# Gated feed-forwards that take the unnormalised residual, with token factor and shift applied behind the PSUM banks

## The reference, cut to what matters

```python
for l in range(DEPTH):                       # DEPTH = 2, SEQ = 256, D_MODEL = 1024
    ...
    y = hybrid_mixer(h, positions, ...)
    x = x + g_m * rms_norm_2(y, mix_norm_post[l])
    h = rms_norm_2(x, ffn_norm_pre[l]) * (1.0 + sc_f) + sh_f
    y = swiglu(h, w_gate_up[l], w_down[l])   # FFN_HIDDEN = 2816
    x = x + g_f * rms_norm_2(y, ffn_norm_post[l])

def rms_norm_2(x, w):
    return x * lax.rsqrt(jnp.mean(x * x, axis=-1, keepdims=True) + EPS) * w

def swiglu(h, w_gate_up, w_down):
    g, u = jnp.split(h @ w_gate_up, 2, axis=-1)
    return (jax.nn.silu(g) * u) @ w_down
```

## Time and profile before

| | |
|---|---|
| median of 3 runs | 2164.08 us (2161.91 to 2165.92) |
| the profiled execution's own time | 2163.82 us |
| its span in the trace | 2161.9 us |
| PE busy | 2004.4 us, 93% |
| DVE busy | 1521.2 us, 70% |
| ACT busy | 907.6 us, 42% |
| POOL busy | 142.3 us, 7% |
| mean granted TensorE clock | 0.959 of full speed |

### The profile page before, as it was taken

The page is one execution under the profiler, slowest core; times in us unless marked ns, Lnnn a source line. Parts: engine busy times, 40 slices in busy tenths (PEclk is TensorE's granted clock), DMA queues, the critical chain, the costliest instruction groups (busy, mean ns, idle before and its releaser), DMA issues. The chain is left out here.

```text
span 2161.9 us, 39923 instructions
## 1 busy us (share of the span) xinstructions
PE 2004.4 (93%) x16706; PEld 1788.0 (83%) x16706; DVE 1521.2 (70%) x2353; ACT 907.6 (42%) x1355; POOL 142.3 (7%) x231
## 2 busy tenths in 40 slices
PE   6998988999999889899999999799899979999997
PEld 5786765788888678798888999789789979988997
DVE  6866557798777668765647787689776667966454
ACT  2435453222222244423225444456544345554443
POOL 0100000001010001201210000000000000000000
PEclk7999989999999989999999999799999999999999
DMA  8542013356453176200004777343358744323552
GB/s 326 203 145 78 2 59 136 136 176 213 161 200 145 58 255 211 104 4 3 3 3 156 250 269 272 127 165 126 136 189 285 270 152 157 136 99 120 192 177 95
DMA packets 59132, 323.92 MB, mean 150 GB/s; under 512 B 6384, under 2 KB 7536, under 8 KB 32624
## 3 DMA queue, kind: packets, MB, share of 16 engines
q1 hardware_dynamic: 33360, 228.97, 29.7%
q0 software_dynamic: 25344, 92.29, 12.0%
q10 hardware_dynamic: 288, 0.66, 0.1%
HBM read 320.84 MB, written 1.05 MB: 149 GB/s over the span
## 5 line engine op out<-in xcount | busy, mean ns | idle before, releaser
L370 DVE TENSOR_TENSOR w_low<-raw,w_high 128x1024 fp32r<-128x1024 f32 (+1 forms) x408 | 473.4, 1202 | 196.9 <-ACT w_high L362 196.7
L362 ACT ACTIVATE w_high<-raw 128x1024 fp32r<-128x1024 f32 (+1 forms) x408 | 402.6, 1034 | 363.0 <-PE banks L407 352.3
L548 DVE SCALAR_TENSOR_TENSOR mod_rows<-mod_rows,silu_condition 128x1024 f32<-128x1024 f32 x176 | 212.9, 1221 | 9.0 <-DMA mod_rows<-rows_dram 6.3
L405 PE MATMUL banks<-ffn_a_l,w_high 128*128 128x256 f32 x704 | 201.1, 286 | 8.5 <-DVE ffn_a_l L712 6.5
L406 PE MATMUL banks<-ffn_a_h,w_high 128*128 128x256 f32 x704 | 199.3, 283 | 0.0
L407 PE MATMUL banks<-ffn_a_h,w_low 128*128 128x256 f32 x704 | 199.1, 283 | 0.0
L534 POOL DMA_DIRECT2D mod_rows<-rows_dram x176 | 93.2, 530 | 1329.7 <-DVE mod_rows L548 1108.6
L405 PE MATMUL banks<-mlp_hidden_l,w_high 128*128 128x512 f32 (+1 forms) x512 | 174.7, 341 | 3.9 <-DVE mlp_hidden_l L1102 3.0
L407 PE MATMUL banks<-mlp_hidden_h,w_low 128*128 128x512 f32 (+1 forms) x512 | 174.5, 341 | 0.0
L406 PE MATMUL banks<-mlp_hidden_h,w_high 128*128 128x512 f32 (+1 forms) x512 | 174.4, 341 | 0.0
L405 PE MATMUL banks<-mix_l,w_high 128*128 128x256 f32 (+1 forms) x448 | 134.4, 300 | 14.0 <-DVE mix_l L759 12.9
(11 more groups left out here) (617 smaller groups left out, 4983.3 us busy)
## 6 DMA issues: line engine op xcount, KB each, us to landing
raw<-panels_dram SPq DMA_DIRECT2D x204, 1024.0 KB, 4.8
mod_rows<-rows_dram POOLq DMA_DIRECT2D x176, 512.0 KB, 5.1
mod_0a_rows<-rows_dram SPq DMA_DIRECT2D x8, 1024.0 KB, 19.3
x_features<-x_features_dram SPq DMA_DIRECT2D x1, 2048.0 KB, 11.2
constants<-small_dram SPq DMA_DIRECT2D x1, 1672.5 KB, 6.7
silu_condition<-conditions_dram SPq DMA_DIRECT2D x2, 512.0 KB, 12.4
out_dram<-x_features SPq DMA_DIRECT2D x4, 256.0 KB, 2.1
constants<-small_dram SPq DMA_DIRECT2D x1, 736.5 KB, 5.1
```

Source lines behind the costliest of these rows:

```text
L362: self.nc.scalar.activation(self.wh[:, m % 2, cols], self.raw[:, slot, cols], ACT.Copy).then_inc(self.w_high, 1)
L370: self.nc.vector.tensor_tensor(self.wl[:, m % 2, cols], self.raw[:, slot, cols], self.wh[:, m % 2, cols].bitcast(F32), ALU.subtract).then_ ...
L405: self.nc.tensor.matmul(out, sh(k), ml(k), start=(opens and k == 0), stop=False)
L548: nc.vector.scalar_tensor_tensor(row if v == nv - 1 else self.scratch[:], row, 1.0, self.cond[v][:], ALU.mult, ALU.mult, accum_out=mod[:, ...
```

## The change

For each gated feed-forward:

- `norm_modulate` ahead of it goes. A `Deferred` object prepares the operand: ACT writes `x * gain` rounded to the high part and squares x, DVE writes the low part. Its small gain and shift work is done beside the first `mix_out` panel.
- In `post_add` POOL does the 8 products `y * r`; DVE keeps the 8 additions to x and does the 8 low parts between them. The two halves of the second panel's split go into `post_add` too.
- The matmuls have 258 columns. In chunk 0 PE goes block by block through both banks of the gate panel and sums the squares of x between them; then it does the up panel. DVE multiplies both halves by `r` on the way out of the banks, ACT adds the gate's shift in the silu, DVE adds the up half's shift in the product.
- Banks 5 to 7 are opened ahead of `post_add`'s sums, bank 4 (which the sums use first) after up(1).
- In the first layer `row_work` is cut into 4 and 28 rows, so that POOL's products stand between them.

The diff, cut to its core:

```diff
+        def pe_up_gated_first(pe):
+            d, ms = deferred, [m_of["up", 0, u] for u in range(2)]
+            with_x = ((0, 0), (0, 1))
...
+            for k in range(KD):
+                pe.wait_ge(d.split, k + 1)
+                for u, b in with_x:
+                    last = half_product(0, ms[u], u, b, k, k == 0, k == KD - 1)
...
+                d.pe_sum(pe, k, 4)
+            self.wait_split(pe, ms[1])
+            for b in range(len(with_x) - 2, 2):
+                for k in range(KD):
+                    last = half_product(0, ms[1], 1, b, k, k == 0, k == KD - 1)
+            last.then_inc(up_done, 1)
...
+        def dve_up_gated(dve, cs, q=None):
...
+            dve.wait_ge(up_done, 2 * c + 1)
+            nc.vector.tensor_copy(bias[:], ps[:, 0:2, n:n + 1]).then_inc(bias_ready, 1)
+            nc.vector.tensor_tensor(act_buf[:], ps[:, 0:2, 0:n], spread(deferred.r[:], 1, 2),
+                                    ALU.mult).then_inc(scaled_ready, 1)
+            dve.wait_ge(up_done, 2 * c + 2)
+            nc.vector.tensor_copy(up_bias[:], ps[:, 2:4, n:n + 1]).then_inc(up_bias_ready, 1)
+            nc.vector.tensor_tensor(hid[:], ps[:, 2:4, 0:n], spread(deferred.r[:], 1, 2),
+                                    ALU.mult).then_inc(up_scaled, 1)
...
+            for b in range(2):
+                last = nc.vector.scalar_tensor_tensor(hid[:, b, :], hid[:, b, :], up_bias[:, b, :], act_buf[:, b, :],
+                                                      ALU.add, ALU.mult)
...
             def body(pe, cs, q):
                 pe_up(pe, cs + 1, q)
+                if deferred is not None and gated and cs == 0:
+                    pe.wait_ge(deferred.rooted, 1)
+                    self.open_sums(pe, (4,))
                 pe_down(pe, cs, q)
...
+            if deferred is not None and gated:
+                self.split_upto("dve", dve, first + 1)
+                deferred.dve_rstd(dve)
+            if deferred is None or not gated:
+                self.split_upto("dve", dve, first + ups)
+            dve_up(dve, 0)
             self.split_upto("dve", dve, first + ups)
-            dve_up(dve, 0)
...
+            @pr.block.gpsimd
+            def _(pool):
+                for w in r_ready:
+                    pool.wait_ge(*w)
+                for k in range(KD):
+                    nc.gpsimd.tensor_tensor(scaled[:, k, :], y[:, k, :], r[:, 0, :], ALU.mult).then_inc(normed, 1)
...
+                pr.open_sums_first()
+                post_add(pr, "mix_post", out_y[:], [], mod, 16, norm("mix_post", l), 4, out_sq,
+                         squared=(squared, (folded, 5), [6, 0, 7]), operand=operand)
...
-                pr.open_sums_first()
-                a_ready = pr.norm_modulate("ffn_pre", norm("ffn_pre", l), mod, 1, 24, 32, TL, high, low,
-                                           lambda k: [(added[0][0], k + 1)], bank=3, scaled_x=y, split_first=1)
```

More of the change, by code:

```diff
@@ L979, in feed_forward, with half_product @@
         up_banks = lambda cs: slice(0, 2) if cs == 0 else slice(first_bank, first_bank + 2)
+        up_scaled, up_bias_ready = (self.sem(f"{name}_{s}") if deferred is not None and gated else None
+                                    for s in ("up_scaled", "up_shift_product_ready"))
+        up_bias = self.sb(f"{name}_up_shift_product", [P, 2, 1], ctx=tmp) if gated else None
+        def half_product(cs, m, u, b, k, first, last):
+            d, out = deferred, ps[:, 2 * u + b, 0:n + 2]
+            cols = slice(k * PC + b * P, k * PC + (b + 1) * P)
+            nc.tensor.matmul(out, self.wh[:, m % 2, cols], d.low[:, k, :], start=first, stop=False)
+            nc.tensor.matmul(out, self.wh[:, m % 2, cols], d.high[:, k, :], start=False, stop=False)
+            return nc.tensor.matmul(out, self.wl[:, m % 2, cols], d.high[:, k, :], start=False, stop=last)
@@ new lines, in pe_up_gated @@
+        def pe_up_gated(pe, cs, q=None):
+            if cs == 0:
+                pe_up_gated_first(pe)
+                return
+            c, d = cs if q is None else q * per + cs, deferred
+            for u in range(2):
+                m = m_of["up", cs, u]
+                self.wait_split(pe, m, q)
+                pe.wait_ge((scaled_ready, up_scaled)[u], c)
+                pe.wait_ge((bias_ready, up_bias_ready)[u], c)
+                for b in range(2):
+                    for k in range(KD):
+                        last = half_product(cs, m, u, b, k, k == 0, k == KD - 1)
+                last.then_inc(up_done, 1)
@@ L2744, in _ @@
                                                    ALU.add).then_inc(ready, 1)
+                if operand is not None and step > 1:
+                    operand.dve_low(dve, step - 2)
+            if operand is not None:
+                operand.dve_low(dve, KD - 1)
+                pr.split_half_dve(dve, 1, 1)
     return [(ready, KD)]
@@ L3510, in squares_behind, with beside_out @@
                                                         ALU.add).then_inc(folded, 1)
+                operand = Deferred(pr, "ffn_pre", pr.xT[:, :, 0:TL], norm("ffn_pre", l), mod, 24, 32, TL, t)
+                def beside_out(which, eng, p):
+                    if which == "dve":
+                        take(eng, 1)
+                    if which == "dve" and p == 0:
+                        operand.dve_begin(eng)
+                    if which == "act" and p == 0:
+                        operand.act_begin(eng, y_split[0])
@@ L3518, in second @@
-            with ExitStack() as t:
-                y = pr.sb("ffn_y", [P, KD, TL], ctx=t)
-                high = pr.sb("ffn_a_h", [P, KD, TL], F32R, ctx=t)
-                low = pr.sb("ffn_a_l", [P, KD, TL], F32R, ctx=t)
-                pr.open_sums_first()
-                a_ready = pr.norm_modulate("ffn_pre", norm("ffn_pre", l), mod, 1, 24, 32, TL, high, low,
-                                           lambda k: [(added[0][0], k + 1)], bank=3, scaled_x=y, split_first=1)
-                sums, sums_ready = pr.feed_forward("ffn", FFN // 256, True, TL, high, low, a_ready, y, [],
-                                                   (lambda eng, point: take(eng, 1)) if l == 0 else None)
+                          beside=beside_out, behind=squares_behind)
```

82 lines of the change are left out of this document (64 added, 18 removed).

## The result

The changed kernel takes 2179.75 us (median of 5 runs, 2177.08 to 2185.05) against 2162.91 for the kernel before (5 runs, 2160.98 to 2165.92). The ratio of their times is 1.0075, 95% interval 1.0062 to 1.0088: slower by about 16 us. The forecast was 2172.6 with a range up to 2179.5. The sign is right; the time lies just beyond the upper edge, and the added time is 16 instead of 8.8.

The account below looks back on a forecast made before the run. PE, busy 93%, and its waits were taken as the bound. Per layer -1.1 + 1.7 (clock behind the stall) + 0.9 + 1.0 + 1.9 = 4.4, both layers 8.8, on 2163.82 gave 2172.6 us; range 2166 to 2179.5.

Parts of the forecast that it names:

- The openings ahead of the sums: Before the mixer's sums: opening banks there takes 2.5 against 0.75 before, making everything behind 1.75 us late.
- E+4.6: Forecast start of the mixer's reciprocal, 4.6 us after E, the end of `mix_out`.
- POOL's contention: Reciprocal to PE's start: POOL products at 0.81 each, DVE operations stretched from 0.40 to 0.6; PE starts at 9.2.
- strict turns: Upper bound for PE's start: POOL and DVE alternate, PE starts 10.1 after `mix_out` ends, the sum 1.8 higher.
- The rival in which POOL keeps ahead: POOL's eight products hold off DVE; PE starts 3.2 later per layer, 15.2 in all, 2179.0 us; chance 0.15.
- Gate panel and clock: Chunk 0's gate panel: 9.35 us at full clock, plus 1.7 for half of one low-clock stretch of 3.4.
- The late split: Before chunk 1: DVE's split waits for the up panel; PE idles 4.2 instead of 0.9, plus 1.7 low clock.
- 258 columns: Two more columns per panel cost 0.05 on 20 panels from chunk 1 on: 1.0 us per layer.
- The first layer's turns: Between chunks: DVE's and ACT's work of 11.2 fits PE's 11.43, nothing charged; a 0.3 miss costs 3.
- The last down panel: At the last chunk: DVE's list grows from 2.07 to 3.96, so PE's last down panel starts 1.9 later.
- the clock did not stay up: Rival at PE's start: clock stays up and nothing is stretched; +1.2 in all, 2165.0 us; chance 0.14.
- the last one: Rival before chunk 1: the late split doesn't hold PE, idle under about 1.5; 2162.6 us; chance 0.08.

Follow-up runs that it names:

- the last kernel: As sorted, DVE, but with openings of all 128 rows and bank 4's opening done three times in PE's wait; 2146.57 us, ratio 0.9933.
- products on DVE: The changed kernel, but DVE does the mixer's eight products again and the 32 rows are issued in one lot; 2180.63 us, ratio 1.0071.
- sorted, DVE: Changed kernel with banks 5-7 opened behind sums, bank 4 behind reciprocal, split and taking out earlier, x sums in bank 3, DVE products; 2152.77 us, ratio 0.9950.

## Why the prediction was right in sign and half in size

Term by term, the first layer's measure and the second's:

- **The openings ahead of the sums: mis-sized, the largest miss.** I charged 1.75 and took the sums at their old length. The reciprocal came at E+5.3 and E+6.75 instead of E+4.6. With the openings behind the sums, or with all rows in them, the sums are back at 1.5. So 0.7 and 2.1 belong to a low clock during openings and sums that I had not counted at all.
- **POOL's contention: mis-sized; the upper bound was right.** From the reciprocal to PE's start I took 4.6; it is 5.4 in both layers, and strict turns gave 5.5. By the Trainium skill (SBUF — State Buffer, "SBUF: two separate sides"), whose lock makes the loser wait for the whole instruction, the sum was to be 1.8 higher; the trace agrees, with 1.6. The rival in which POOL keeps ahead has nearly the right time, 2179.0, for a wrong reason: POOL and DVE alternate, 0.87 each.
- **Gate panel and clock: right, in part by luck.** 11.05 forecast, 10.6 and 10.7 measured. I had taken a low stretch of 3.4 of its own; what ran at 0.50 here, 3.2 and 3.6, was the end of the stretch that began with the openings.
- **The late split: right.** Up panel, stall, low clock, chunk 1 and the opening of bank 4 were 24.0 in the sum and take 24.2 and 24.3. Undoing the split alone gave back 10.8 of 16.3.
- **258 columns: right.** The second layer's nine turns take 154.55 against 153.36, 1.2 instead of 1.0.
- **The first layer's turns: wrong.** I had 0.2 of slack and charged nothing. The turns take 2.6 more than before, where the second layer's take 1.2 more, and with the gate half taken out earlier the two layers are equal. The prediction had named this as the way to fail on the bad side.
- **The last down panel: right, and its clock missed.** 1.9 forecast, 1.97 measured in both layers. Behind it the last panel of the second layer takes 7.5 instead of the first layer's 6.0, at the lower clock level, which I had charged only behind the longer stall.

Misses of 4.4 at PE's start, 1.8 in the turns and 1.65 at the end, less 0.4 in between, make up the 7.5 by which the stretches exceed the sum. Of the 4.4, 2.8 is the clock during openings and sums and 1.6 the turns with POOL. The other two rivals fell: the clock did not stay up and DVE's operations were stretched, and PE idle ahead of chunk 1 was 4.04, far over the 1.5 of the last one.

The change itself was not the loss. In the last kernel its idea, operands that need no norm, together with the clock that is kept up, is worth 8.3 and 8.4 us at down(0) (34.7 and 34.6 instead of 43.0); the order of a few steps around it, and the low clock that their waits and openings brought, turned that into a loss.

## What to carry to other kernels

When an edit takes a wait off one engine, follow the in-order list of the engine that feeds it: a split that used to lie in a gap may now stand behind the wait that replaced the gap, and moving it cost nothing here. Idle time of PE has a second price, the lower clock behind it, which falls on work that is now ready; work that started earlier inside such a stretch gained about half in one pair of kernels (products on DVE) and all of it in another (sorted, DVE), where the stretch itself came out shorter. A slack of a few tenths in a loop may not hold, and a miss counts in every turn.

## What was not expected of the hardware

- Openings with one row let the granted clock fall (0.59, then 0.50, while PE was busy without a pause); the same openings with 128 rows kept it at 1.00. One-row openings put into PE's wait did not keep it up (0.50 over the last 3.2 of 5.25). Full-row matmuls that add zeros, put into that wait, kept it up to its end and over the panel behind it.
- A wait of 1.97 ahead of the last down panel was followed by the lower level in one of the two layers in each of six kernels (last two panels 15.3 instead of 13.8), now the first, now the second; the waits of 0.92 in three kernels never were, and the waits of 4.04 ahead of chunk 1 in six kernels always were. What decides between the two layers stays open.
